# The output-gate products of the first block's recurrence, given out as dense steps between the units of its attention

## The reference

```
def first_block(x, ...):
    h = rms_norm(x, ln1_g[i])
    z = h @ w_in[i]
    mq, mk, mv, mo, mi, mf, aq, akc, avc, aks, avs, akw, avw, ag = jnp.split(z, offs, axis=-1)
    hm = mlstm(mq.reshape(mshape), mk.reshape(mshape), mv.reshape(mshape), ...)
    hm = rms_norm(hm, mlstm_norm_g[i].reshape(M_HEADS, M_HEAD_DIM)).reshape(B, S, M_WIDTH)
    m_out = (hm * jax.nn.sigmoid(mo.astype(jnp.float32))).astype(x.dtype)
    a_out = nsa(aq..., akc, avc, aks, avs, akw, avw, ag, ...)   # 3 branches, softmax each, gated sum
    x = x + jnp.concatenate([m_out, a_out], axis=-1) @ w_out[i]
    x = x + conv_ffn(rms_norm(x, ln2_g[i]), ...)
    gate = jax.nn.sigmoid(rms_norm(x, ple_norm_g[i]) @ w_ple_gate[i])
    x = x + gate * (p[i] @ w_ple_proj[i])
```

## Time and profile before

| | us |
|---|---|
| median of 3 runs | 1615.57 (1615.27 to 1616.48) |
| the profiled execution, own time | 1616.05 |
| its span in the trace | 1614.8 |
| PE busy | 1552.9 (96%) |
| DVE, ACT, POOL busy | 882.8, 636.8, 48.7 |
| mean granted TensorE clock, share of full | 0.994 |
| PE's share of the chain that ended last | 88% |

### The profile page before, as it was taken

How to read it: one execution, slowest core, us unless ns; L and a number is a source line. 1 busy time by engine, 2 the same in 40 slices (tenths; PEclk the granted TensorE clock), 3 DMA queues, 4 the chain that set the end, 5 groups by cost and what they waited for, 6 DMA issues and landing times.

```text
span 1614.8 us, 24777 instructions
## 1 busy us (share of the span) xinstructions
PE 1552.9 (96%) x10341; PEld 1333.9 (83%) x10341; DVE 882.8 (55%) x1592; ACT 636.8 (39%) x1134; POOL 48.7 (3%) x50
## 2 busy tenths in 40 slices
PE   7999979999999999999999899999999999999997
PEld 5898866678888888899998788999998987678886
DVE  4435656666645655875554554446664454554443
ACT  5233346543322343744344443223343343542333
POOL 0000001000000000020000000000020000000000
PEclk9999999999999999999999999999999999999999
DMA  6232300033323332432112102224431113013231
GB/s 196 84 83 54 103 14 14 27 106 102 105 86 97 104 103 80 106 72 72 53 53 53 53 23 71 92 79 142 82 79 53 53 53 65 28 40 107 89 118 53
DMA packets 168192, 123.05 MB, mean 76 GB/s; under 512 B 48640, under 2 KB 163840, under 8 KB 168080
## 3 DMA queue, kind: packets, MB, share of 16 engines
q1 hardware_dynamic: 168080, 121.46, 26.4%
HBM read 119.35 MB, written 2.10 MB: 75 GB/s over the span
## 4 chain that ended last, share of the span: by engine, by line
PE 88%; DVE 5%; ACT 4%; issue 2%; POOL 0%; DVEq 0%; ACTq 0%; POOLq 0%
PE bank L581 69%; PE bank L2798 2%; PE bank L2764 2%; PE bank L2778 2%; DVE w_lo L541 1%; PE bank L3174 1%; ACT w_hi L532 1%; PE bank L2668 1%; PE bank L1650 1%; PE bank L1593 1%; PE bank L2619 1%; PE bank L1469 1%; PE bank L3137 1%; PE bank L3153 1%; ACT probs L1523 1%
## 5 line engine op out<-in xcount | busy, mean ns | idle before, releaser
L541 DVE TENSOR_TENSOR w_lo<-w_raw,w_hi 128x2048 fp32r<-128x2048 f32 (+2 forms) x117 | 241.1, 2061 | 167.8 <-ACT w_hi L532 167.2
L581 PE MATMUL bank<-h_hi,w_hi 128*128 128x512 f32 (+2 forms) x920 | 323.6, 372 | 6.0 <-DVE w_lo L541 2.2
L581 PE MATMUL bank<-h_hi,w_lo 128*128 128x512 f32 (+2 forms) x920 | 317.6, 365 | 0.0
L581 PE MATMUL bank<-h_lo,w_hi 128*128 128x512 f32 (+2 forms) x920 | 317.3, 365 | 0.0
L532 ACT ACTIVATE w_hi<-w_raw 128x2048 fp32r<-128x2048 f32 (+2 forms) x117 | 201.0, 1719 | 64.9 <-DMA w_raw<-w_in 28.9
L581 PEld LDWEIGHTS bank<-h_hi,w_hi 128*128 128x128 f32 (+1 forms) x920 | 165.7, 189 | 42.7 <-issue 12.9
L581 PEld LDWEIGHTS bank<-h_hi,w_lo 128*128 128x128 f32 (+1 forms) x920 | 165.5, 188 | 28.3
L581 PEld LDWEIGHTS bank<-h_lo,w_hi 128*128 128x128 f32 (+1 forms) x920 | 165.6, 188 | 26.7 <-issue 0.5
L581 PE MATMUL bank<-g_hi,w_hi 128*128 128x264 f32 (+1 forms) x752 | 181.3, 307 | 1.5 <-DVE z_a L2217 0.9
L581 PE MATMUL bank<-g_hi,w_lo 128*128 128x264 f32 (+1 forms) x752 | 178.7, 303 | 0.0
L581 PE MATMUL bank<-g_lo,w_hi 128*128 128x264 f32 (+1 forms) x752 | 178.7, 303 | 0.0
(11 more groups left out here) (593 smaller groups left out, 2614.9 us busy)
## 6 DMA issues: line engine op xcount, KB each, us to landing
w_raw<-w_in SPq DMA_DIRECT2D x45, 1024.0 KB, 5.2
w_raw<-w_up SPq DMA_DIRECT2D x32, 512.0 KB, 5.2
w_raw<-w_in SPq DMA_DIRECT2D x40, 256.0 KB, 4.5
w_raw<-w_down SPq DMA_DIRECT2D x8, 1024.0 KB, 5.2
w_raw<-w_out SPq DMA_DIRECT2D x8, 1024.0 KB, 5.1
w_raw<-w_out SPq DMA_DIRECT2D x8, 512.0 KB, 3.4
w_raw<-w_ple_gate SPq DMA_DIRECT2D x4, 1024.0 KB, 5.0
w_raw<-w_o_attn SPq DMA_DIRECT2D x8, 512.0 KB, 3.4
```

The costliest lines, as they stand in the source:

```text
L541: DV.e.tensor_tensor(wlo[u % RING][:, 0:n], raw[u % RING][:, 0:n], whi[u % RING][:, 0:n].bitcast(F32), ALU.subtract).then_inc(*w_low(u))
L581: ins = PE.e.matmul(out, stationary[a](k), moving[b](k)[i], start=first and n == 0, stop=last and n == 2)
```

## The change

The eight `mo` steps leave the recurrence's rest and become the first eight fill steps of the attention; after them comes one empty step, then `m feat` and `mix m` as before, so 20 of 21 fill steps are spread over the 26 units. The two `mo` weight units move behind the key and value units in the fetch order. The gating by DVE leaves the end of the recurrence and becomes `dv_mlstm_gate`, one tile in each of the sixth to ninth fill steps. The recurrence keeps its 24 steps, but only 18 steps of rest; nothing stands beside steps 18 to 23. `a_features` moves to memory of its own, since `mo` and `mq` now live on. On ACT, the copy of the first unit's factors moves from the turning of unit 0 to that of unit 1.

```diff
--- before.py
+++ after.py
...
@@ -460,12 +461,13 @@
 
         w_in = A["w_in"]
         plan(w_in, 0, KT, [(Z_MI, Z_MI + 32), (Z_MI + MH, Z_MI + MH + 32), (Z_AG - 8, Z_AG + 3 * AH)])
-        plan_cols(w_in, Z_MQ, Z_MI)
+        plan_cols(w_in, Z_MQ, Z_MO)
         plan(w_in, 0, KT, [(Z_KC, Z_KC + 2 * KW)])
         for a, w1 in enumerate(("cmp_k_w1", "cmp_v_w1")):
             plan(w_in, 0, KT, head_pairs(Z_AQ, a))
             units.append(([(0, CH, A[w1].rearrange("(k p) n -> p k n", p=P))], CB // 2, CH, False))
         plan_cols(w_in, Z_KS, Z_AG)
+        plan_cols(w_in, Z_MO, Z_MI)
         first_unit = {"mix_out": len(units)}
         for half_k in (0, 4):
             plan_cols(A["w_out"], 0, D, k0=half_k, kts=4)
@@ -1217,18 +1219,19 @@
                     yield
             DV.wait_ge(*hm_squared.at(MH * TT - 1))
             DV.e.tensor_scalar(msq[:, 1, :, :], msq[:, 0, :, :], 4.0 / MD, 4.0 * EPS, ALU.mult, ALU.add).then_inc(*den_step("mean"))
-            for a in range(2):
-                for t in range(TT):
-                    DV.wait_ge(*evac.at("mo", a, t))
-            hm_v = mqT[:, :, :].rearrange("p h (t d) -> p t h d", t=TT)
             for t in range(TT):
                 yield
-                if t == 0:
-                    DV.wait_ge(*mroot_made.at())
-                g = mo[:, t, :].rearrange("p (h d) -> p h d", h=MH)
-                DV.e.scalar_tensor_tensor(g, g, 1.0, hm_v[:, t, :, :], ALU.add, ALU.mult).then_inc(*den_step("gated", t))
-                DV.wait_ge(*den_step.at("gated", t))
-                DV.e.tensor_tensor(g, g, msq[:, 0, t, :].unsqueeze(2).broadcast_to([P, MH, MD]), ALU.mult).then_inc(*mo_made(t))
+
+        def dv_mlstm_gate(t):
+            if t == 0:
+                DV.wait_ge(*mroot_made.at())
+            for a in range(2):
+                DV.wait_ge(*evac.at("mo", a, t))
+            g = mo[:, t, :].rearrange("p (h d) -> p h d", h=MH)
+            hm_t = mqT[:, :, t * P:(t + 1) * P]
+            DV.e.scalar_tensor_tensor(g, g, 1.0, hm_t, ALU.add, ALU.mult).then_inc(*den_step("gated", t))
+            DV.wait_ge(*den_step.at("gated", t))
+            DV.e.tensor_tensor(g, g, msq[:, 0, t, :].unsqueeze(2).broadcast_to([P, MH, MD]), ALU.mult).then_inc(*mo_made(t))
 
         def po_mlstm_root():
             PO.wait_ge(*den_step.at("mean"))
@@ -1336,8 +1339,6 @@
         kv_keys = [("kv", j) for j in range(2)]
 
         def pe_rest_steps():
-            for a in range(2):
-                yield from pe_tokens_steps(dense_1, ("mo", a), tiles1, H1)
             yield from pe_features_steps(dense_1, kv_keys, S, H1)
             compress = pe_compress_steps()
             yield from rest_order(compress, [pe_features_steps(dense_1, aq_keys(a), S, H1) for a in range(2)])
@@ -1360,9 +1361,6 @@
                 yield
 
         def ac_rest_steps():
-            for a in range(2):
-                yield from ac_tokens_steps(("mo", a), tiles1, mo_at(a), lambda t: var[:, 6, t:t + 1], lambda: half_root.at(),
-                                           func=ACT.Tanh)
             yield from ac_splits(kv_keys)
             compress = ac_compress_steps()
             yield from rest_order(compress, [ac_splits(aq_keys(a)) for a in range(2)])
@@ -1378,11 +1376,6 @@
                 yield
 
         def dv_rest_steps():
-            for a in range(2):
-                for t in range(TT):
-                    if t == TT - 1:
-                        dv_split()
-                    yield
             yield from dv_scaled_steps("ln1", kv_keys, [kvT[:, j, :] for j in range(2)], S, row_1)
             compress = dv_compress_steps()
             yield from rest_order(compress, [dv_scaled_steps("ln1", aq_keys(a), [aqT[:, 2 * a + j, :] for j in range(2)], S, row_1,
@@ -1430,7 +1423,7 @@
         per_bank = [4, 2, 1, 1]
         units_n = [u for t in range(TT) for u in [(t, 0, 0)] + [(t, br, j) for br in (1, 2) for j in range(0, 4, per_bank[t])]]
         number_n = {u: i for i, u in enumerate(units_n)}
-        dense_n, dense_6 = ring(*[0] * 11, 6), ring(0, 1, 2, 3, 4, 5)
+        dense_n, dense_6 = ring(*[0] * 19, 6), ring(0, 1, 2, 3, 4, 5)
         n_scored, n_taken, n_soft = signal(PE, "n_scored"), signal(DV, "n_taken"), signal(DV, "n_soft")
         n_exp, n_turned = signal(AC, "n_exp"), signal(PE, "n_turned")
         n_flip_a, n_flip_d = signal(AC, "n_flip_a"), signal(DV, "n_flip_d")
@@ -1605,7 +1598,7 @@
         def ac_nsa_turn(unit):
             i = number_n[unit]
             dst, src = flip(unit, 0)
-            if i > 1 and is_last(units_n[i - 1]):
+            if i and is_last(units_n[i - 1]):
                 ac_nsa_factors(units_n[i - 1])
             if i > 1:
                 AC.wait_ge(*n_valued.at(i - 2))
@@ -1613,7 +1606,6 @@
             AC.e.activation(dst, src, ACT.Copy).then_inc(*n_flip_a(i, 0))
             if i == 0:
                 ac_nsa_wide(unit)
-                ac_nsa_factors(unit)
 
         def ac_nsa_widen(unit):
             i = number_n[unit]
@@ -1677,6 +1669,11 @@
                 DV.e.tensor_tensor(total, total, of_branch, ALU.add).then_inc(*n_out(t, br, "added"))
 
         def pe_mlstm_out_steps():
+            for a in range(2):
+                yield from pe_tokens_steps(dense_n, ("mo", a), tiles1, H1)
+            yield
+            for t in range(TT):
+                PE.wait_ge(*mo_made.at(t))
             for k in range(4):
                 b = pe_bank(dense_n, "m feat", k)
                 for t in range(TT):
@@ -1686,6 +1683,11 @@
             yield from pe_residual_steps(dense_n, "mix m", h_of("m"), 4, S)
 
         def ac_mlstm_out_steps():
+            for a in range(2):
+                yield from ac_tokens_steps(("mo", a), tiles1, mo_at(a), lambda t: var[:, 6, t:t + 1], lambda: half_root.at(),
+                                           func=ACT.Tanh)
+            yield
+            AC.wait_ge(*product.at("mo", 1, TT - 1))
             for k in range(4):
                 if k > 1:
                     AC.wait_ge(*h_high.at("m", k - 2))
@@ -1697,6 +1699,12 @@
             yield from ac_residual_steps("mix m", S)
 
         def dv_mlstm_out_steps():
+            for n in range(2 * TT + 1):
+                if n % TT == TT - 1:
+                    dv_split()
+                if n > TT:
+                    dv_mlstm_gate(n - TT - 1)
+                yield
             for k in range(4):
                 yield
             yield from dv_residual_steps("mix m", S)
@@ -1716,7 +1724,7 @@
         def pe_nsa():
             fence(PE, "mlstm")
             fill = pe_mlstm_out_steps()
-            filled(units_n, first_steps(fill, 11), 11, pe_nsa_score, pe_nsa_turn, pe_nsa_value, apart=True)
+            filled(units_n, first_steps(fill, 20), 20, pe_nsa_score, pe_nsa_turn, pe_nsa_value, apart=True)
             for t, br, j0 in units_n[-2:]:
                 PE.wait_ge(*n_taken.at(t, br, heads_of((t, br, j0))[-1][2]))
             drain(fill)
@@ -1730,7 +1738,7 @@
                         stage_(units_n[step - behind])
                 if step > 2:
                     value(units_n[step - 3])
-                while given < 11 * min(step, len(units_n)) // len(units_n):
+                while given < 20 * min(step, len(units_n)) // len(units_n):
                     next(fill)
                     given += 1
 
```

3 lines of the change are left out of this document (2 added, 1 removed).

## The result

The kernel after takes 1640.09 us (median of 4, 1639.41 to 1645.06) against 1615.88 (1615.27 to 1616.48) for the kernel before: ratio 1.0156, 95% interval 1.0136 to 1.0177. It is slower, as forecast, but by 24.2 us where 14.9 were forecast (1630.5 against the median of 1615.57 that was known then), and 1.1 us above the range of 1619 to 1639. The profiled execution took 1639.7 us, its span is 1638.4.

A forecast was written before the change was run, and what follows sets the result against it. PE was taken to set the time. Idle of 10.0, 4.7 and 2.0 us plus 1.4 of clock made 18.1, less 3.1 gave 15.0; 1616.05 + 15.0 = 1631.05, less 0.5 against the median: 1630.5, range 1619 to 1639.

The forecast's parts named there:

- deduction of 3.1: Recurrence and attention: 3.1 us of the forecast waits are work already there, at 0.14 us a step for switching groups.
- the longer wait for v_features: Sign in the recurrence: PE's turning of v waits for v_features longer than the 2.67 us of before.
- Recurrence, plus 10.0: Recurrence: 14.1 us of PE idle (3.2 + 4.9 + 1.1 + 4.9) for 4.1 before, so plus 10.0 us.
- the tail: Recurrence's end: steps 18 to 23 hold no product, so PE waits 4.9 us for the chain through POOL's root.
- The wait for a weighing: Recurrence, scores of step 12 and the sums: PE waits for DVE's weighings, 3.2 us of idle.
- the first turning of v: Recurrence after step 13: PE reaches the turning of v at 32.9 and waits to 37.8, 4.9 us.
- Attention's start, plus 4.7: Attention's first eight steps, token tiles 0 and 1: 12.8 us of idle for 8.1 before, so plus 4.7 us.
- The loop: Attention's start: one bank ties fill, turning and ACT's late tanh; gate steps wait 4.6, 1.3, none, 3.4, 0.7 us.
- Tiles 2 and 3, plus 2.0: Attention, token tiles 2 and 3: 5.5 us of idle for 3.5 before, so plus 2.0, between 0 and 5.
- cancels: DVE's gating, like the gate products and tanhs, leaves the recurrence and comes back in the attention, for no net cost.
- Clock, plus 1.4: Recurrence and attention: four low stretches at 1.4 us each against three, so plus 1.4, between minus 2.8 and plus 8.
- The third rival: Token tiles 0 and 1: clock stays at 1.2 GHz through gate steps, 6 us more, 1637 or 1640; chance 0.2.

The follow-up runs named there:

- e1: The kernel after, with the attention's first PE, ACT and DVE instructions no longer waiting for POOL's root; 1640.8 us.
- e2: The kernel after, with ACT doing its fill work (the tanh or the copy of m feat) first in each attention step instead of last; 1629.1 us.
- e5: e2 with DVE's gating of each token tile one fill step earlier; 1622.9 us.
- e4: The kernel before, with only ACT's copy of the first unit's factors moved behind the second unit's exponentials; 1616.7 us.
- e3: The kernel after, plus 36 unused products on PE between the last sums and the attention's first scores, where it waits for the root; 1642.3 us.
- e7: The kernel after, with all eight gate products back in the recurrence as its last dense steps, gating in the attention's first four fill steps; 1622.8 us.
- e8: The kernel after, with four gate products as the recurrence's last dense steps, four in the attention, tanh first, gating in fill step t; 1621.2 us.
- e11: e5 with e1's edit, so the attention's start doesn't wait for POOL's root; 1621.0 us.
- e9: The kernel before, with DVE's gating moved into the attention's first four fill steps and e4's edit, products left in place; 1619.8 us.
- e10: e8 with its four recurrence gate products as the first dense steps instead of the last; 1619.4 us.

## Why the prediction was off

**The sum.** The four terms gave 16.7 us of idle and 1.4 of clock, less a deduction of 3.1: 15.0. Measured are 16.3 us of idle, 6.7 of PE busy for longer, and 0.8 ahead of the recurrence, 23.9 in all. The sum of the idle was right by luck: its parts, 10.0, 4.7 and 2.0, came as 4.9, 2.4 and 9.0. The miss of 8.9 us is then the clock (5.3), the deduction (3.1) and the 0.8 that no edit made, less 0.4 of idle. Of the signs that it named, the wait for the tanh, the first scores near 199 (197.3) behind the root, and the number of low stretches came true; the longer wait for v_features didn't (1.1 us), and the attention lasted 162.5 us for a forecast of about 148.

**Recurrence, plus 10.0: measured plus 4.9.** This is idle time alone. Of its four waits, the tail is right (4.9 us for the root; measured 4.7, and e1 shows that waiting for the root and not only for the mean squares costs 2.4 of them). The wait for a weighing is nearly so (3.2; 1.7 + 0.8). The step that failed is the first turning of v: 4.9 us against 1.1. The kernels with the same recurrence show 2.5 to 2.9 us there (e1: 2.93). From its start the turning comes after the same time in after and in e1 (76.8 us), so 1.8 us of the wait were hidden in the kernel after by the low clock from 157 on, which made PE late. The other 2 us fit the bound that the prediction named, steps of DVE that overlap better than I added them; that wasn't tried by itself.

**Attention's start, plus 4.7: measured plus 2.4.** The loop is as walked: 4.6, 1.3, 0, 3.4, 0.7 us of waits for the tanh were forecast, 3.70, 1.10, 0, 3.06 and 0.59 are in the trace, and 0.42 once more. e2 shows it by taking it away. The term is smaller than forecast since in this stretch these waits are 8.5 us for 10.0 (the last one falls into tile 2) and the others 2.0 for 2.8. The Trainium skill, Perfetto Trace Analysis, Matmuls under Optimizing Tensor Performance, advises to rotate independent groups through different PSUM banks so that emptying overlaps the next group. The trace agrees in so far as the one bank cost 8.9 us of waits. But e2 removed them without a second bank, by the order of the engine that empties it; no run here gave the gate steps a second one.

**Tiles 2 and 3, plus 2.0: measured plus 9.0.** The step that failed is the sentence that the gating "cancels". Its 1.4 us a tile do, its place doesn't. Before, it ended 5.6 us ahead of the attention's first scores; after, the last one is the ninth fill's, and `m feat` needs it. It stood behind the eighth tanh at 276.21, the split, the tile before, two reads of scores and a copy: 4.67 us of wait. e2 left 3.0 of it, and e5 removed those and made the attention 4.1 us shorter. The additions to X behind the values cost 3.2 us for my 2.4, the copies of m features 1.0, not foreseen.

**Clock, plus 1.4: measured 6.7.** The number of low stretches was inside what I named, five. The step that failed is that each was priced at the length of those of before, 3.4 us: four of the five lasted 6.8, and the low clock lasted 20.4 us longer in all, where the forecast had 3.4. For the one length the price holds: 3.4 us cost 1.6 in the recurrence (before against e4), and 1.3 to 2.3 behind the end, where the programs are the same (1280.2 to 1280.9 us in e3, e4, e7, e8 and e11 for 1278.6 to 1278.9). A stretch of 10.2 us in the second block cost 3.5 to 3.9 (1282.4 us in e2 and e9, 1282.5 in e1). In e1 it looks like this, PE busy and the clock at half:

```profile
1395.00:1406.00 11.00, 10.72 (x39) 8.41 (x40) 4.94 (x18) 6.07 (x20) 0.00 (x0) 0.57 0.02 5
```

That is mostly 0.35 to 0.5 us for each us, and 0.67 at most (e3). But a part of the low clock after fell into waits: PE was busy in it for 13.2 us more than before. A gate step's matmuls start 0.12 us apart, at half clock 0.21 (211.31, 211.53, 211.74 and so on in the second step). They so lose 0.44 of the time, my estimate; 13.2 us make 5.8 of the 6.7.

The deduction of 3.1 us for switching between groups isn't shown by any run; the sum of the idle can't test it, with parts that are off by up to 7 us. Without it the sum would have been 18.1. The third rival, low clock in the gate steps, has the right time (1637 to 1640) and the right place in two of five stretches: the second and fifth gate steps took 4.9 and 4.4 us for 3.0, the other six ran at full clock, and the stretches at 158, 195 and 281 lie elsewhere.

**What the runs say of the change as a whole.** With the two orders mended and the root off the start (e11) the move still costs 4.4 us of length, and 5.1 in the median. Taking the products from the head of the recurrence costs 5.5 us there (e7 against e9), 2.8 of them waits; the rest goes with a low stretch, and one execution of each can't say whether it belongs to the order. And the attention, which has 8.1 us of idle in its start, took the products in for little less than their own time at best: from first scores to end, e5 takes 145.8 us and e11 145.3, where 122.7 and 23.0 make 145.7; with half of the products e10 takes 132.6 for 134.2. PE's waits in it are 11.2 us before and 10.3 in e5: nearly nothing of its idle time was filled. I read it as the latency of its own chain, exponentials and factor copies, which moves behind what is put in front of it; no run isolates that.

Why the attention of e7 and e9 takes 2.6 to 3.0 us more than before with no product in it can be read in part. Against e4, which has the same order of factor copies and the same 10.2 us of low clock, e9 takes 3.1 us more and waits 2.9 more: 0.9 for the copies of m features and 0.9 for the additions to X, which the 15 fill steps pushed back and for which neither before nor e4 waits, 0.5 for the inverse and 0.6 for the factor copies (7.6 us for 7.0). The gating in DVE's queue was not tried without the shift.
